# Token halves in the stages on both sides of a norm, with the steps of the norm placed between their chunks

## What is computed

```python
h = x
# first block
h = h + mixers(rms_norm(h, ln_mix_g)) @ w_out      # dilated and stick-breaking attention, gated
h = h + memory_cross_attn(rms_norm(h, ln_x_g), rms_norm(mem, ln_mem_g), ...)
h = h + conv_gated_mlp(rms_norm(h, ln_ffn_g), w_up, conv_w, conv_b, w_down)   # D_FF = 2816
h = rms_norm(h, ln_f_g)
# two more layers; each part lies between two norms, "pre" and "post"
#   h = h + 0.5 * rms_norm(swiglu(rms_norm(h, pre)), post)        feed-forward, twice a layer
#   h = h + rms_norm(gmlp(rms_norm(h, pre)), post)                mixer of layer 0
#   h = h + rms_norm(rwkv7(rms_norm(h, pre)), post)               mixer of layer 1
#   h = h + rms_norm(sigmoid(rms_norm(h, pre) @ w_gate) * (p @ w_proj), post)   embedding part
def rms_norm(x, g):
    y = x * rsqrt(mean(x * x, axis=-1) + eps)
    return y * g
```

## Time and profile before

| | |
|---|---|
| median of 3 runs | 4235.42 us (4219.64 to 4237.18) |
| profiled execution, its time | 4230.84 us |
| profiled execution, its span | 4229.0 us |
| mean granted TensorE clock | 0.889 |
| PE busy | 3670.3 us, 87% |
| DVE busy | 1851.5 us, 44% |
| ACT busy | 1167.1 us, 28% |
| read from memory | 279.07 MB, 66 GB/s |

### The profile page before, as it was taken

The page is one execution under the profiler, slowest core; times in us unless marked ns, Lnnn a source line. Parts: engine busy times, 40 slices in busy tenths (PEclk is TensorE's granted clock), DMA queues, the critical chain, the costliest instruction groups (busy, mean ns, idle before and its releaser), DMA issues. The chain is left out here.

```text
span 4229.0 us, 50513 instructions
## 1 busy us (share of the span) xinstructions
PE 3670.3 (87%) x22482; PEld 2958.7 (70%) x22482; DVE 1851.5 (44%) x2268; ACT 1167.1 (28%) x1423; POOL 0.2 (0%) x4
## 2 busy tenths in 40 slices
PE   7888579779998999869899978999687677689996
PEld 6656357658877887868788867887466666478874
DVE  5222223547734333454433244333646774743334
ACT  2222432332222222323322223222333231232222
POOL 0000000000000000000000000000000000000000
PEclk9758789869998999889899988999888987789997
DMA  3001012202222222212122311222120000012221
GB/s 134 30 0 60 0 50 100 70 30 100 93 90 77 100 84 95 100 50 100 60 100 88 102 65 60 100 85 66 62 78 28 3 3 12 31 69 100 85 90 40
DMA packets 43273, 284.40 MB, mean 67 GB/s; under 512 B 4785, under 2 KB 4913, under 8 KB 16817
## 3 DMA queue, kind: packets, MB, share of 16 engines
q1 hardware_dynamic: 43056, 281.18, 19.3%
HBM read 279.07 MB, written 2.10 MB: 66 GB/s over the span
## 5 line engine op out<-in xcount | busy, mean ns | idle before, releaser
L392 PE MATMUL ps<-xh,wh 128*128 128x512 f32 x2688 | 1065.2, 396 | 68.1 <-DVE xl L1502 33.9
L392 PE MATMUL ps<-xl,wh 128*128 128x512 f32 x2688 | 1059.6, 394 | 0.0
L392 PE MATMUL ps<-xh,wl 128*128 128x512 f32 x2688 | 1058.2, 394 | 0.0
L289 DVE TENSOR_TENSOR wl<-raw,wh 128x2048 fp32r<-128x2048 f32 (+3 forms) x284 | 591.6, 2083 | 557.7 <-ACT wh L284 556.7
L392 PEld LDWEIGHTS ps<-xh,wh 128*128 128x128 f32 x2688 | 511.7, 190 | 202.2 <-issue 83.5
L284 ACT CAST wh<-raw 128x2048 fp32r<-128x2048 f32 (+3 forms) x284 | 493.0, 1736 | 417.8 <-PE ps L392 412.6
L392 PEld LDWEIGHTS ps<-xh,wl 128*128 128x128 f32 x2688 | 511.3, 190 | 110.0 <-issue 1.5
L392 PEld LDWEIGHTS ps<-xl,wh 128*128 128x128 f32 x2688 | 512.3, 191 | 107.8 <-issue 0.8
L392 PE MATMUL ps<-hid_h,wh 128*128 128x512 f32 x880 | 347.1, 394 | 1.1 <-DVE wl L289 1.1
L392 PE MATMUL ps<-hid_h,wl 128*128 128x512 f32 x880 | 347.0, 394 | 0.0
L392 PE MATMUL ps<-hid_l,wh 128*128 128x512 f32 x880 | 347.0, 394 | 0.0
(11 more groups left out here) (301 smaller groups left out, 4025.8 us busy)
## 6 DMA issues: line engine op xcount, KB each, us to landing
raw<-in_up SPq DMA_DIRECT2D x88, 1024.0 KB, 4.9
raw<-in_down SPq DMA_DIRECT2D x64, 704.0 KB, 4.1
raw<-in_up_c SPq DMA_DIRECT2D x22, 1024.0 KB, 4.9
raw<-in_down_c SPq DMA_DIRECT2D x16, 704.0 KB, 4.0
raw<-in_gates SPq DMA_DIRECT2D x8, 1024.0 KB, 4.8
raw<-in_gv SPq DMA_DIRECT2D x8, 1024.0 KB, 4.9
raw<-in_gu SPq DMA_DIRECT2D x8, 1024.0 KB, 4.9
raw<-in_gout SPq DMA_DIRECT2D x8, 1024.0 KB, 4.9
```

The costliest lines, as they stand in the source:

```text
L289: nc.vector.tensor_tensor(wl[:, slot, 0:w], raw[:, slot, 0:w], wh[:, slot, 0:w].bitcast(F32), ALU.subtract).then_inc(lo_ready, 1)
L392: last = nc.tensor.matmul(out, stationary, moving, start=(fresh and q == 0), stop=(t == kt - 1 and half == per - 1 and q == 2), skip_group ...
```

## The change

Stages on both sides of a norm are made by halves of 256 tokens, `HALVES`. A down stage, gout, rout and ple_gate are streamed twice over, first for tokens 0 to 255 ("a"), then for tokens 256 to 511 ("b"). An up stage and gv do this for the first six chunks only (`LEAD`), the others stay whole. All matmuls, evictions and sums of such a stage are 256 tokens wide (gv: two token blocks instead of four).

A norm becomes a `Chain` of twelve numbered steps for one half of the tokens. A stage that is given a chain (`along`) calls it at fixed places, its hooks: PE after every 24 to 33 matmuls, ACT and DVE between the split of the next chunk and the eviction of the unit. Chain 0 runs along the b half of the stage before the norm, chain 1 along the a half of the stage behind it. What is left of a chain's steps stands in `rest`. The second norm of a chain now sums its squares on DVE and not on PE. In the embedding part ple_proj comes before ple_gate and is stored, and its operand is loaded and split before the feed-forward (`embedding`). Ahead of rwkv chain 1 stands alone. The output is stored by halves. `linear` now evicts at most two output tiles at a time; stages with four or eight have more units for it.

```diff
+LEAD = 6
...
+def by_halves(name, width, count):
+    return [(name + "a", name, width, range(count)), (name + "b", name, width, range(count))]
+def halves_first(name, width, count):
+    return [(name + "a", name, width, range(LEAD)), (name + "b", name, width, range(LEAD)),
...
+STREAM += stage("up_c", 2048, KF) + by_halves("down_c", DOWN, 2 * KD)
+STREAM += halves_first("up_00", 2048, KF) + by_halves("down_00", DOWN, 2 * KD)
+STREAM += halves_first("gv", 2048, 8) + stage("gu", 2048, 8) + by_halves("gout", 2048, 8)
+STREAM += halves_first("up_01", 2048, KF) + by_halves("down_01", DOWN, 2 * KD)
...
+        hooks = max(1, blocks * kt // 8)
...
+        at_hook = along.at if along else 0
+        if along:
+            along.at += units * per * hooks
...
+            hook = at_hook
+            for unit in range(units):
+                for half in range(per):
+                    n = a + unit // lots * per + half + 1
+                    if unit % lots == 0 and n < len(order):
+                        split_hi(act, n, 16 * (n // 2 + 1), n % 2, order[n][2])
+                    if along:
+                        for _ in range(hooks):
+                            along.act(act, hook)
+                            hook += 1
+                if act_part:
+                    wait_products(act, unit)
+                    act_part(act, unit, outputs(unit), side(unit))
...
+                    pairs = ([(m, t) for t in range(kt) for m in range(blocks)] if lead else
+                             [(m, t) for m in range(blocks) for t in range(kt)])
+                    for n, (m, t) in enumerate(pairs):
+                        if lead and m == 0:
                             norms.wait_tile(pe, t + half * kt)
-                            for m in range(blocks):
-                                last = multiply(0, half, m, t, t == 0 and half == 0 and bank(0, m)[1] == 0)
-                    else:
-                        for m in range(blocks):
-                            if m == 4 and lots == 2:
-                                pe.wait_ge(psum_read.sem, psum_read.base + unit * lots)
-                            for t in range(kt):
-                                last = multiply(unit, half, m, t, t == 0 and half == 0)
-                    last.then_inc(chunks_used, 1)
+                        last = multiply(unit, half, m, t, t == 0 and half == 0 and not (lead and bank(unit, m)[1]))
+                        if n + 1 == len(pairs):
+                            last.then_inc(chunks_used if unit % lots == lots - 1 else lot_done.sem, 1)
+                        if along and ((n + 1) % (len(pairs) // hooks) == 0 or n + 1 == len(pairs)):
+                            along.pe(pe, hook)
+                            hook += 1
+    def evicted(engine):
...
+    class Chain:
+        SUM, ROOT, APPLY, SUM_2, ROOT_2, WRITE, END = 0, 1, 2, 5, 6, 7, 12
+        def __init__(self, half, *passes):
+            self.passes = [Pass(n, by="vector" if n else "before", tokens=HALVES[half], **p) for n, p in enumerate(passes)]
+            self.one, self.two = (self.passes + [None])[0:2]
+            self.at = 0
+        def pe(self, pe, step):
+            if step == self.SUM:
+                self.one.sum_up(pe)
+            elif step == self.ROOT:
+                self.one.spread(pe)
+            elif step == self.SUM_2 and self.two:
+                self.two.sum_up(pe)
+            elif step == self.ROOT_2 and self.two:
+                self.two.spread(pe)
+        def act(self, act, step):
+            if step == self.ROOT:
+                self.one.square_root(act)
+            elif self.APPLY <= step < self.APPLY + 4 and self.two:
+                for t in range(2 * (step - self.APPLY), 2 * (step - self.APPLY) + 2):
+                    if t == 0:
+                        self.one.wait(act, n_spread, 1)
+                    self.two.square(act, t, self.one)
+            elif step == self.ROOT_2 and self.two:
+                self.two.square_root(act)
+            elif self.WRITE <= step < self.WRITE + 4 and self.two and self.two.split:
+                for t in range(2 * (step - self.WRITE), 2 * (step - self.WRITE) + 2):
+                    self.two.high(act, t)
+        def dve(self, dve, step):
+            if step == self.ROOT:
+                self.one.invert(dve)
+            elif self.APPLY <= step < self.APPLY + 4:
+                t = 2 * (step - self.APPLY)
+                self.one.value(dve, t)
+                self.one.value(dve, t + 1)
+                self.one.finish(dve, t)
+                self.one.finish(dve, t + 1)
+                if self.two:
+                    if t:
+                        self.two.sum_squares(dve, t)
+                    self.two.sum_squares(dve, t + 1)
+            elif step == self.ROOT_2 and self.two:
+                self.two.invert(dve)
+            elif self.WRITE <= step < self.END and self.two:
+                t = 2 * (step - self.WRITE)
+                if t:
+                    self.two.finish(dve, t - 2)
+                    self.two.finish(dve, t - 1)
+                if t < KD:
+                    self.two.value(dve, t)
+                    self.two.value(dve, t + 1)
+        def rest(self):
+            @block.tensor
+            def _(pe):
+                for step in range(self.at, self.END):
+                    self.pe(pe, step)
+            @block.scalar
+            def _(act):
+                for step in range(self.at, self.END):
+                    self.act(act, step)
+            @block.vector
+            def _(dve):
+                for step in range(self.at, self.END):
+                    self.dve(dve, step)
+            self.at = self.END
+        def wait_tile(self, pe, t):
+            self.passes[-1].wait_result(pe, t)
...
+    class Ready:
+        def __init__(self, chain):
+            self.wait_tile = chain.wait_tile
...
+    def down(name, move, target, tiles_made, *passes):
+        for half in range(2):
+            along = None
+            if half:
+                along = Chain(0, *passes)
+            linear(name + "ab"[half], HALF, P, hid_split, halves=True, norms=None if half else Made(tiles_made),
+                   along=along, **summing(move(HALVES[half]), target, 1, HALVES[half]))
+        return along
+    def up_onto(name, chain, *passes):
+        chain.rest()
+        for half in range(2):
+            other = Chain(1, *passes) if half == 0 else other
+            linear(name + "ab"[half], KD, 256, x_split, norms=Ready(other if half else chain), along=None if half else other,
+                   **swiglu(0, HALVES[half]))
+            if half == 0:
+                other.rest()
+        linear(name, KD, 256, x_split, **swiglu(LEAD))
+    def feed_forward(layer, n, chain, passes, *next_passes):
+        up_onto(f"up_{layer}{n}", chain, *passes)
+        return down(f"down_{layer}{n}", lambda tokens: to_tiles(ybuf, 1, tokens=tokens), ybuf,
+                    lambda t: max(0, 2 * (t - LEAD) + 2), *next_passes)
...
+    def embedding(layer):
         p_here = fetch([(pt[:, :, :], io[f"p{layer}"])], f"p{layer}", multiplied)
...
+        other = Chain(1, *passes)
+        linear(f"ple_proj{layer}", 2, D, pt_split, norms=Ready(made), dve_part=to_tiles(proj, 2), along=other)
+        @block.vector
+        def _(dve):
             evicted(dve)
-        linear(f"ple_proj{layer}", 2, D, pt_split, norms=Halves(pt, 2, pt_split),
-               **summing(proj_part, ybuf, KD))
-        pending.append((ybuf, gain(layer, 7)))
-    def gmlp():
+        linear(f"ple_gate{layer}a", KD, 256, x_split, norms=Ready(chain), along=other, **gated(HALVES[0]))
+        other.rest()
+        along = Chain(0, *next_passes)
+        linear(f"ple_gate{layer}b", KD, 256, x_split, norms=Ready(other), along=along, **gated(HALVES[1]))
+        return along
...
+        other = Chain(1, *passes)
+        linear("gva", KD, 256, x_split, norms=Ready(chain), along=other, **gated_values(0, 0))
+        other.rest()
+        linear("gvb", KD, 256, x_split, norms=Ready(other), **gated_values(0, 1))
+        linear("gv", KD, 256, x_split, **gated_values(LEAD))
...
+        Chain(1, post(ybuf, 1, 1), dict(source=h, gain=gain(1, 2), plain=hn)).rest()
...
+        for n, part in enumerate((chain, last)):
+            part.wait_tile(sp, KD - 1)
+            sp.dma_start(io["out"][:, :, HALVES[n]], h[:, :, HALVES[n]]).then_inc(stored, 16)
+        sp.wait_ge(stored, 32)
```

More of the change, by code:

```diff
@@ L1304, in _ @@
             p_here(act)
+            made.act(act)
         @block.vector
@@ L1548, in part @@
             def part(act, unit, products, u):
-                for m in range(KD):
-                    last = nc.scalar.activation(buf[:, m, :], products[m], ACT.Sigmoid, bias=col(bias, m))
-                    if m % 4 == 3:
-                        last.then_inc(psum_read.sem, 1)
+                for m in range(2):
+                    last = nc.scalar.activation(buf[:, 2 * unit + m, :], products[m], ACT.Sigmoid,
```

(2 more changed lines are left out.)

545 lines of the change are left out of this document (315 added, 230 removed).

## The result

The changed kernel takes 4269.98 us (4266.44 to 4272.43, 4 runs), the kernel before beside it 4228.86 us: ratio 1.0097, 95% interval 1.007 to 1.0124. It is slower by 1%. The forecast was 4300 us, slower by 1.5%. The profiled execution took 4266.44 us, its span is 4264.7 us (before 4229.0), so the sum to be explained is +35.7 us. The mean granted clock is 0.905 (before 0.889).

The account below looks back on a forecast made before the run. PE bounds it, busy 87% with norm holes of about 33 us. Saved 187.5, paid 235.5, less 9: net +39; clock +25; span 4229.0 + 64 = 4293, so 4300 us (+1.5%). Range 4120 to 4395.

Parts of the forecast that it names:

- the last two rows of the table: Inside rwkv from lw to rout, and everything ahead of down_c: forecast difference 0 for each.
- the clock's term: One PE resumption at half rate in each of 15 stages with a chain, 1.7 us each: +25 us.
- the loads of p: Embedding: ACT and DVE wait for p's load in front of the next stage, 4 us, twice: 8 us paid.
- The joins: Norm holes between down_c/up_00, down_00/gv and gout/up_01: three at 33 us, 98 us saved.
- The walk through a hooked up stage: Up stage, chain beside its a half: a half 52 us, b half 36, 88 against 65.3 for whole chunks, +23.
- PE's wait in front of the second sum: Sign of being right: in the up a halves PE waits some 10 us before the second pass's sum.
- The down stages: Five down stages streamed twice, chain beside the b half: 142 against 123 us, +19 each, 95 in all.
- spaced by more than 120 ns: Sign of being wrong: matmuls of 256 tokens start more than 120 ns apart.
- rout to up_11: From rout's start to up_11: 78 us before, 65 after, -13 us.
- the clock staying down in the hooked stages: Rival: clock stays low in hooked stages, 15 x 8 = +120 us, 4395; clock or further cost above 4350, chance 0.17.
- The rival that the chains hide in DVE's idle time: Chain steps fit DVE's idle time in stages, only unhooked loops cost: 248 us saved, 4040; partly or well hidden, 0.25.
- The matmuls' width: Twice as many matmuls, 256 instead of 512 wide, cost PE -20 to +40 us in all, taken as next to nothing.

Follow-up runs that it names:

- e1_two_tiles: The kernel before with only the eviction of at most two tiles at a time, no halves and no chains; 4196.76 us, ratio 0.9929.
- e9_p_behind_up: Changed kernel with DVE's steps before splits, twelve half-width chunks per up-stage pass, ACT's root before wh; here p is split behind the up stage; 4166.93 us, 0.9858.
- e4_sum_later: The changed kernel with PE's second sum moved one step later, right ahead of the second spread; 4287.95 us, ratio 1.0143 to before.
- e3_step_first: The changed kernel with a chunk's first chain step ahead of the next chunk's split on DVE, not behind it; 4190.37 us, ratio 0.9913 to before.
- e2_no_hooks: The changed kernel with halves kept but chains run alone between them, except in the ple stages; 4362.42 us, ratio 1.0317 to before.

## Why the prediction was right, point by point

**The sign and the size.** Forecast +64 us of span, measured +35.7. The difference of 28 has two parts: 21.7 us are the last two rows of the table, which the forecast set at nothing. All the rest came to +56 against 64. The missing 8 us can be put down to the clock's term, 17 us instead of 25, if the loads of p and the first block's savings are taken as forecast; that is a remainder and was not measured by itself.

**The step that was mis-sized** is one that the prediction does not have. The diff lets `linear` evict at most two tiles at a time, and I gave it no cost and no gain, nor did I look at the stages with four and eight tiles. It measured -31.5 us alone (e1_two_tiles), with lg2's 9.2 in it. Some 13 lie in the embedding parts, which the forecast had worked out at their new length anyhow. Of the 21.7 that were missed, 9.2 are lg2 at the high clock, which neither the forecast nor the edit aimed at, and about 12 are the evictions. The trace of before showed these: a stage's DVE idle for 21.93 us and then busy with evictions. That lg2 ran fast in this execution brought the time further from the forecast, not nearer.

**The joins** (98 saved, measured 92): the holes left are 0.35, 0.57 and 0.12 us, under the 2 us given. The 1.6 us of clock behind each hole, which is in the 33, is in the stages in the table.

**The walk through a hooked up stage** held within some 4 us. It had PE resume behind SUM_2 at 27.9 us, the second root at 34.0, the b half at 52.1. up_00 measured 26.7, 31.6 and 49.8; up_01, with the load and split of p in front of its second chunk, 31.8, 36.7 and 55.5. e9_p_behind_up bears the load out: without it the second chunk of up_01 starts at 6.1 us instead of 10.0. But up_10 has no load of p and is as late as up_01 (31.7, 36.6, 54.8). There ACT rounds the last tiles of xh (L575), what was left of chain 0's steps, until 2587.6, and only then makes the wh of the second chunk, 4.7 us after the stage's start at 2582.93 (4.8 in up_01, 2.0 in up_00):

```profile
2587.60 1.90 ACT L310 CAST wh<-raw 128x2048 fp32r<-128x2048 f32 x1
```

The forecast had 2.5 us for this late split, in the embedding part. The b halves took 36.3, forecast 36. The four up stages cost 19.3, 24.9, 24.1 and 25.3 us, in sum 93.6; forecast were 23 each, 8 for the loads of p in up_01 and up_11, and 1.7 each for the clock. Of the signs that I named, PE's wait in front of the second sum came, but with 6.4 to 7.2 us instead of some 10, since PE finished chunk 2 later than walked (23.8 us in up_01, forecast 18.1). A second wait in front of the spread hardly came, 0.5 us in up_00, 0.3 in up_10 and none in up_01 and up_11: PE worked through 24 matmuls at half clock instead.

**The down stages** (+89.4, forecast 95): the a half took 65 to 65.5 us in four of the five, two chunks in 7.96 to 8.1, forecast 8.0. The reason given, the splits' loop, is what the trace shows. The second chunk of each pair waits for its wl; DVE and then PE in down_00's a half, by time:

```profile
1612.28 1.62 DVE L315 TENSOR_TENSOR wl<-raw,wh 128x1408 fp32r<-128x1408 f32 x1 [0.84 <-ACT wh L310]
```

```profile
1613.49 0.28 PE L436 MATMUL ps<-hid_h,wl 128*128 128x256 f32 x1
1613.96 0.39 PE L436 MATMUL ps<-hid_h,wh 128*128 128x256 f32 x1 [0.20 <-DVE wl L315]
```

wl ends at 1613.90 and PE's next chunk starts 0.06 us later, as at every second chunk of this half. PE's margin is small all the same. The stretch view of the change has 455 matmuls in 55 us:

```profile
1575.00:1630.00 55.00, 54.07 (x455) 52.68 (x453) 27.82 (x28) 20.08 (x21) 0.00 (x0) 1.00 0.55 183
```

These 121 ns each include the waits; inside the chunks of this half the matmuls start 113 to 121 ns apart, 116 on average, where I had 117. The sign "spaced by more than 120 ns" did not come true here, and only just not in the up b halves (119.9). All the steps between chunks together are 3.4 to 4.1 us a half longer than a matmul's, so no more than that can be gained there by a faster split. down_c's a half took 70.0 us, which the forecast, with one length for all five, did not have: PE waits 4.87 us for its second chunk, whose wl comes behind the convolution of up_c's last unit.

**rout to up_11** (-13, measured -4.8): the one term that failed outright. The working was 9 us for the first chunk, 17 for the rest of routa, 36 for routb, 3 behind it; measured 13.1, 19.0, 37.8 and 3.0. The first chunk did not get shorter with half the tokens: 13.1 us in both. By time, DVE in it:

```profile
3682.88 3.35 DVE L2374 RECIPROCAL tmp<-tmp 128x512 f32<-128x512 f32 x1
...
3689.22 0.69 DVE L2388 TENSOR_TENSOR xl<-tmp,xh 128x512 fp32r<-128x512 f32 x1 [0.68 <-ACT xh L2352]
```

The norm by heads still makes all 512 tokens of its last tile before PE may multiply any of them. I had counted products and not looked at what releases them. The row that I took for rout's first matmul is its second; the first starts at 3657.18, so rout took 45.6 us before and not 44.4.

**The clock** (+25, 1.7 us for each of 15 resumptions): chunk 1 of up_01a took 7.45 us instead of 5.82, 1.6 of loss, and from the first to the last of the 24 matmuls behind the sum it was 5.05 instead of 2.8. The size is right. The number on the path should be smaller than 15, since in the change the second kind lies in time that PE waits anyway; that it can go otherwise e4_sum_later shows. Of the rivals, the clock staying down in the hooked stages was wrong: it was 0.87 over up_01's hooked a half, 0.93 over up_00's and 0.96 over down_00's hooked b half. Over the whole kernel it went up, from 0.889 to 0.905.

**The rival that the chains hide in DVE's idle time** was set low for the right reason: they stand in order between split and eviction. e3_step_first moved one of them and nothing else, and the kernel fell by 80 us, 5.3 for each of the 15 hooked stages on average. The prediction put the turning point at 4.3 less each; the kernel did turn from slower to faster. But e3_step_first is only 6 us under e1_two_tiles, which has neither halves nor chains, and their intervals overlap, so the halved norm in that order just earns its own cost. In e9_p_behind_up it earns 30 us.

**The matmuls' width** (next to nothing, -20 to +40): inside a chunk 119.9 ns for products of xh, where I had 113, and 116 for hid. By these spacings a pair costs 13 ns more in an up stage and 2 ns less in a down stage than the one that it replaces, which lies in the range. In the b halves of the up stages PE's own 5.8 us a chunk, not the loop's 5.64, is the limit; that 36 us came out there is in part luck.

Not tried: other widths than 256 tokens, and steps of one tile.

## What to carry to other kernels

Work put "beside" other work in an in-order queue costs nothing only if it stands where its engine waits for something outside: ahead of the instruction that has the wait, not behind it. Walk the loop from the end of one chunk to the readiness of the next but one, and place the step in the link in which its engine is idle; here that was worth 80 us, while thinning the steps out cost some 9 us in one order and at most 7 were gained by it in the other. And cost every edit in a diff, the helper's small rewrite too: here the kernel with it alone was 31 us faster, two fifths of what the rest of the change lost, though 9 of these are a stage's clock.

## What the runs showed of the hardware

- Inside a chunk matmuls of 256 columns start 119.9 ns apart on average for products of xh (up_00's b half) and 116 for hid (down_00's a half, between 113 and 121); of 512 columns 226.7 and 233.3 ns (up_00 and down_00 of the kernel before). I had taken 113 and 117, from the 111 of the mem stage and the 119.6 of gv.
- In the kernel before, lg2 ran at a clock of 0.56, 23.1 us for 48 matmuls, though PE was busy 95% of that stretch and waited for nothing between them: the first seven start within 1.75 us, as in e1_two_tiles (1.76), and from there on the steps are almost twice as long. In e1_two_tiles it took 13.9 us at 1.00. The stretch views of before and then of e1_two_tiles, each with the 36 us ahead of it:

```profile
3530.00:3566.00 36.00, 22.94 (x698) 21.47 (x694) 14.50 (x23) 3.67 (x4) 0.00 (x0) 0.86 0.01 2
3566.00:3591.00 25.00, 23.72 (x48) 12.39 (x48) 3.07 (x3) 0.00 (x0) 0.00 (x0) 0.56 0.12 43
```

```profile
3514.00:3550.00 36.00, 22.36 (x734) 20.80 (x727) 15.70 (x24) 4.05 (x5) 0.00 (x0) 0.95 0.01 3
3551.00:3566.00 15.00, 14.22 (x48) 7.69 (x48) 6.47 (x8) 0.00 (x0) 0.00 (x0) 1.00 0.22 71
```

  e2_no_hooks, with the same evictions as e1_two_tiles, had the low clock again, 22.9 us for the stage:

```profile
3677.00:3699.00 22.00, 22.00 (x46) 11.54 (x45) 5.11 (x7) 0.00 (x0) 0.00 (x0) 0.54 0.14 48
```

  The change and the seven kernels from e3_step_first on took 13.9. PE's work ahead of it is nearly the same in all; the clock over the 36 us ahead was lower where lg2 was slow (0.86 and 0.81) than in e1_two_tiles (0.95) and the change (1.00). What put the clock down stays open. One profiled execution of each kernel is all that shows it, so the 9 us may differ between executions of one kernel.
- Behind a wait of 3.7 to 9.5 us inside a hooked stage of the change the next ten matmuls of 256 columns start 0.23 us apart on average (0.24 behind the wait of 3.71), and the clock came up again within the chunk or the next (0.12 us apart).
